# Fetching u for the S5 branch from another queue, and the order of VectorE's last steps before it

## Chip, cores and metric

The kernel runs on one core of a Trainium2 chip. The metric is the device time of one execution in microseconds, the median of several. A core has five engines that work side by side, each through its own instructions in order: TensorE (PE in the profile, matmuls), VectorE (DVE), ScalarE (ACT), GpSimd (POOL) and SyncE (SP, which only starts DMAs here). They meet at semaphores. The queue of an engine can also hold instructions that start a DMA; the profile marks SyncE's as SPq.

## What is computed

Two layers of a hybrid decoder trunk over 512 tokens of width 1024. Each layer is half a SwiGLU step, a mixing step with four branches, and another half SwiGLU step. This case plays at the start of mixing, where the normed input h is projected and the S5 branch begins:

```python
h = rms_norm(x, mix_norm[l])
p = h @ w_in[l]
p_m2, p_s5, p_dsa, p_hg = jnp.split(p, IN_SPLITS, axis=-1)
...
def s5_branch(u, ...):                       # u is p_s5, 512 columns in 32 groups of 16
    ug = u.reshape(b, L, S5_GROUPS, S5_GROUP)
    bu_re = jnp.einsum("blgi,gpi->blgp", ug, bb_re)
    bu_im = jnp.einsum("blgi,gpi->blgp", ug, bb_im)
    ...                                      # a scan over time, then y, gelu and a gated product
```

All arithmetic is float32. Each large product is made of three matmuls on split operands: x is written as x_hi + x_lo and w as w_hi + w_lo, with hi rounded to the matmul's own format, and hi times hi, lo times hi and hi times lo are summed.

## The kernel before

**Weight lots.** All weights come as a stream of lots, 512 KB each, numbered through a layer: 68 for the first SwiGLU step (MIX0 = 68), then the lots of mixing, then those of the second SwiGLU step. SP loads lot n into one of four slots of the tile raw (`load_lot`, L1074 in the profile, or the loop `ring`, L1107). ScalarE rounds it to w_hi (`split_hi`, L425). Then w_lo = raw - w_hi is made by VectorE or GpSimd (`split_lo`, L433), which counts `lo_done`; TensorE begins a lot when this count is there (`begin`). `lot_after(n)` on SP waits until lot n-4 has been split, since the slot is then free.

**The order of the steps** is a list, SCRIPT, that each engine's program walks through, doing its own part of each step. It begins: s5_w 0, quad u, s5_w 1, lot ks, lot q0, turn_small, q1, q2, s5_in, q3, k0, s5_out, k1, and so on. Lots: u is MIX0 to MIX0+3, ks MIX0+4, q0 MIX0+5, q1 MIX0+6, q2 MIX0+7.

- **quad u**: TensorE makes four output tiles of u from unnormed x, tile by tile of the eight k tiles. Meanwhile VectorE's `normalise_h` (L1814) makes the normed tiles, ScalarE rounds each to h_hi (L1488) and VectorE makes h_lo of it (`rest`, L1820). Afterwards VectorE reads the four banks of u times rstd into s5_uc (`keep_u`, L1826), with the columns reordered by time step.
- **s5_w 1**: TensorE transposes small matrices (L721), ScalarE copies them to s5_w (L1495), four copies here, eight in all.
- **lot ks** is the first gemm on the normed h: it waits for h_lo tile by tile. ScalarE evacuates its bank in three copies (L1415 to L1417), and the last frees the bank.
- **turn_small** (TensorE, L688): waits until ks is evacuated and until all eight s5_w copies are made, then does four tiny transposes (L693).
- **s5_in** (TensorE, L725): waits for `s5_u_in` (eight fetches of u), for s5_w and for ScalarE's copy of turn_small's result, then runs 128 small matmuls (L733).

**The way of u** over DRAM: SP writes s5_uc, one DMA for each of four tiles (L1150), into s5_ud, and fetches it back in another layout into s5_u, eight DMAs of 128 KB (L1157), one for each of the eight time steps of a block. Before the fetches it waits for all four writes. Two weight lots, MIX0+8 and MIX0+9, are loaded in between: one ahead of fetch 0, one ahead of fetch 4; MIX0+10 and MIX0+11 follow.

**On VectorE** the last steps of `normalise_h` are: keep_u(0), keep_u(1), the w_lo split of lot ks, keep_u(2), keep_u(3), rest(6), rest(7). **On ScalarE** quad ends with the splits of lots n+5, n+6 and n+7 (n = MIX0), and s5_w 1 follows. **GpSimd** in quad waits for the w_lo split of lot ks, then makes w_lo of lots n+5, n+6 and n+7 as their w_hi come.

Of the kernel before, what the change touches and what calls it, by code (L numbers as in the profile page):

```python
# [10 lines left out]
KT = DM // P  # L11
# [7 lines left out]
S5_Q, S5_CH = 8, 64  # L19
# [182 lines left out]
def trunk(nc, x_in, positions, w_lots, par_in, s5_in, con_in, gamma_in, out, s5_taps, s5_ud):  # L202
# [5 lines left out]
    with ctx:  # L208
# [159 lines left out]
        S = {}  # L368
# [58 lines left out]
        def split_lo(eng, n0, it=0):  # L427

            if isinstance(it, int) and n0 >= NLOT and OUT.layer == DEPTH - 1:
                return  # L430
            s = slot(n0)
            eng.wait_ge(S["hi_done"], 4 * it + (n0 + 1 + OUT.layer * NLOT))
            eng.tensor_tensor(w_lo[:, s], raw[:, s], w_hi[:, s].bitcast(f32), SUB).then_inc(S["lo_done"], 1)  # L433
# [633 lines left out]
        @block.sync  # L1067
        def _(sp):

            upper, freq = CON_AT["blk"], CON_AT["invfreq"]  # L1070

            def load_lot(layer, n):
                s = (layer * NLOT + n) % 4
                sp.dma_start(raw[:, s].rearrange("p k m -> p (k m)"), w_lots[layer * NLOT + n]) \  # L1074
                  .then_inc(S["raw_in%d" % s], 16)

            def load_par(layer):
                sp.dma_start(par[:, :], par_in[layer]).then_inc(S["par_in"], 16)

            def load_x(k):  # L1080
                sp.dma_start(x[:, k], x_in[k]).then_inc(S["c_x%d" % k], 16)

            def load_first(k):

                done = S["raw_in%d" % (k // 2)] if k % 2 else S["c_x%d" % k if k else "c_w0"]
                sp.dma_start(raw_k[:, k].rearrange("p j m -> p (j m)"), w_lots[k // 2][:, 4 * P * (k % 2):4 * P * (k % 2 + 1)]) \
                  .then_inc(done, 16)

            load_x(0)
            load_par(0)  # L1090
            load_first(0)
            for k in range(1, KT):
                load_x(k)
                load_first(k)
            sp.dma_start(con[:, 0:upper], con_in[:, 0:upper]).then_inc(S["c_ones"], 16)
            sp.dma_start(pos_i[:, :], positions.partition_broadcast(P)).then_inc(S["c_pos"], 16)
            sp.dma_start(con[:, freq:NCON], con_in[:, freq:NCON]).then_inc(S["c_pos"], 16)
            sp.dma_start(gam[:, :, :], gamma_in).then_inc(S["c_pos"], 16)
            for layer in range(DEPTH):
                OUT.layer = layer  # L1100

                def ring(first, to):
                    with sp.Fori(first, to) as it:
                        for n in range(4):

                            sp.wait_ge(S["lo_done"], it * 4 + LOT(n - 3))
                            sp.dma_start(raw[:, slot(n)].rearrange("p k m -> p (k m)"),  # L1107
                                         w_lots[layer * NLOT + it * 4 + n]).then_inc(S["raw_in%d" % slot(n)], 16)

                def lot_after(n):  # L1110

                    sp.wait_ge(S["lo_done"], LOT(n - 3))
                    load_lot(layer, n)

                def halves_across(g):

                    wait_taken(sp, out_at("qk"[g], 3))
                    for i in range(4):
                        to, of = slice(32 * i, 32 * i + 32), slice(32 * (i ^ 1), 32 * (i ^ 1) + 32)
                        sp.dma_start(da_s[to].rearrange("p j s -> p (j s)"),  # L1120
                                     da_qk[of, 4 * g:4 * g + 4].rearrange("p j s -> p (j s)")).then_inc(S["da_shifted"], 16)

                if layer:

                    sp.wait_ge(S["lo_done"], LOT(4))
                    sp.wait_ge(S["mix_clear"], 1)
                ring(1, 3)
                if layer == 0:
                    sp.dma_start(con[:, upper:freq], con_in[:, upper:freq]).then_inc(S["c_rest"], 16)
                sp.dma_start(s5_bc[:, :, :, :].rearrange("p a b c -> p (a b c)"), s5_in[layer, :, 0:1024]) \  # L1130
                  .then_inc(S["s5_in"], 16)
                sp.dma_start(s5_bp[:, :, :, :].rearrange("p a b c -> p (a b c)"), s5_in[layer, :, 1024:2048]) \
                  .then_inc(S["s5_in"], 16)
                ring(3, MIX0 // 4)
                sp.wait_ge(S["s5_tap_d"], 4)
                taps = s5_taps.rearrange("i (j g) c -> g i j c", g=8)
                for g in range(8):
                    sp.dma_start(taps[g], s5_tap[16 * g:16 * g + 16]).then_inc(S["s5_tap_out"], 16)
                ring(MIX0 // 4, MIX0 // 4 + 2)

                sp.wait_ge(S["s5_tap_out"], 16 * 8)
                sp.wait_ge(S["out_done"], OUT[MIX0])
                for i in range(S5_Q):
                    sp.dma_start(s5_t[16 * i:16 * i + 16], s5_taps[:, :, P - 16 * i:2 * P - 16 * i]) \
                      .then_inc(S["s5_taps_in"], 16)
                turn = FFN2_0 // 4 + 3
                for i in range(4):

                    wait_taken(sp, out_at("u", i))
                    sp.dma_start(s5_ud[P * i:P * (i + 1)], s5_uc[:, i]).then_inc(S["s5_u_out"], 16)  # L1150
                next_lot = MIX0 // 4 * 4 + 8
                sp.wait_ge(S["s5_u_out"], 16 * 4)
                u_by_step = s5_ud.rearrange("(g i) t c -> t i g c", i=16)
                for t in range(S5_Q):
                    if t % 4 == 0:
                        lot_after(next_lot + t // 4)
                    sp.dma_start(s5_u[16 * t:16 * t + 16], u_by_step[t]).then_inc(S["s5_u_in"], 16)  # L1157
                for n in (2, 3):
                    lot_after(next_lot + n)
                ring(MIX0 // 4 + 3, MIX0 // 4 + 4)  # L1160
                next_lot = MIX0 // 4 * 4 + 20
                for n in (-4, -3, -2):
                    lot_after(next_lot + n)
                sp.wait_ge(S["s5_y"], 2)
                halves_across(0)
                for n in (-1, 0, 1):
                    lot_after(next_lot + n)
                sp.wait_ge(S["da_rope"], 4)
                halves_across(1)
                for n in (2, 3):  # L1170
                    lot_after(next_lot + n)
                ring(MIX0 // 4 + 6, turn)

                sp.wait_ge(S["h_done"], H(H_RAW[2] + KT))
                if layer < DEPTH - 1:
                    load_par(layer + 1)
                ring(turn, NLOT // 4)
                for n in range(NLOT // 4 * 4, NLOT):
                    lot_after(n)
                for n in range(NLOT, NLOT + 4 if layer < DEPTH - 1 else NLOT):  # L1180

                    sp.wait_ge(S["lo_done"], LOT(n - 3))
                    load_lot(layer + 1, n - NLOT)
            n = NLOT - KT
            for i in range(KT - 1):
                wait_taken(sp, OUT[n + i])
                sp.dma_start(out[i], x[:, i]).then_inc(S["e_out"], 16)
            for half in range(2):
                tok = slice(2 * P * half, 2 * P * (half + 1))
                wait_taken(sp, OUT[n + KT - 1] + half)  # L1190
                sp.dma_start(out[KT - 1][:, tok], x[:, KT - 1, tok]).then_inc(S["e_out"], 16)
            sp.wait_ge(S["e_out"], 16 * (KT + 1))
# [78 lines left out]
        def _(act):  # L1271
# [203 lines left out]
            def quad(kind, i):  # L1475

                n = LOT_AT[(kind, i)]
                rstd_of(1)
                for k in range(KT):
                    if k == KT - 2:  # L1480
                        split_hi(act, n + 4)
                    act.wait_ge(S["normed_ready"], k + 1)
                    if k < KT - 1:

                        act.wait_ge(S["h_step"], k + 1)
                    else:
                        wait_out(act, OUT[n] + 3)
                    act.activation(h_hi[:, k], normed[:, k % 2], AFT.Copy).then_inc(S["h_hi_done"], 1)  # L1488
                for j in range(1, 4):
                    split_hi(act, n + 4 + j)  # L1490

            def s5_w_(phase):
# [291 lines left out]
        def _(dve):  # L1784
# [29 lines left out]
            def normalise_h():  # L1814
# [20 lines left out]
                keep_u(0)  # L1835
                keep_u(1)
                split_lo(V, MIX0 + 4)
                keep_u(2)
                keep_u(3)
                rest(KT - 2)  # L1840
                rest(KT - 1)

            def ffn(which, nb):
                n, g0 = nb, G(which)
# [718 lines left out]
```

## Time and profile before

| | us |
|---|---|
| median of 3 runs | 2822.57 (2822.3 to 2822.82) |
| the profiled execution | 2822.68 |
| its span in the trace | 2820.9 |
| TensorE busy | 2813.4 |
| VectorE busy | 1590.5 |
| ScalarE busy | 1185.5 |
| GpSimd busy | 707.0 |

The span is the time from the first to the last instruction of the profiled execution; the device time has 1.8 us around it. Busy time counts instructions that compute; register, semaphore and DMA-starting instructions aren't counted. Times of the trace are microseconds from the span's start. The two layers pass the place of the change at about 400 us and at about 1805 us.

### The profile page before, as it was taken

What the parts mean: (1) busy time and instruction counts of PE and PEld (TensorE: products, weight loads), DVE (VectorE), ACT (ScalarE), POOL (GpSimd) and SP (SyncE); (2) the same over time, 40 slices, a digit from 0 to 9 for tenths busy, and PEclk for the clock granted to TensorE, in tenths of its full rate; (3) what the DMA queues carried; (4) which work ended last, traced back from release to release, by engine and by line L of the source; (5) the groups of instructions that cost most, each with busy time, mean ns of one, the idle gap of its engine ahead of it and who ended that gap; (6) DMA issues with size and microseconds to landing.
All of it is one profiled execution on the core that took longest, in us unless ns stands there. A gap on an engine that the chain in (4) does not pass through costs nothing.

```text
span 2820.9 us, 38653 instructions
## 1 busy us (share of the span) xinstructions
PE 2813.4 (100%) x14306; PEld 2301.0 (82%) x14306; DVE 1590.5 (56%) x2316; ACT 1185.5 (42%) x1715; POOL 707.0 (25%) x336
## 2 busy tenths in 40 slices
PE   9999999999999999999999999999999999999999
PEld 8888888877788888888888888887777888888888
DVE  5584557685557454343544845576856673543434
ACT  5342354555355344232443423446553653442322
POOL 0085023333333440000000840234333334400000
PEclk9999999999999999999999999999999999999999
DMA  5333393222222232333233333932222222333332
GB/s 196 97 95 99 105 149 113 77 74 75 75 83 90 85 99 94 98 98 95 97 127 97 95 95 113 152 99 83 75 75 75 83 83 90 96 97 97 96 97 90
DMA packets 94242, 275.73 MB, mean 98 GB/s; under 512 B 17824, under 2 KB 27552, under 8 KB 93600
## 3 DMA queue, kind: packets, MB, share of 16 engines
q1 hardware_dynamic: 94112, 273.95, 33.6%
q8 instruction: 87, 1.43, 0.2%
q14 instruction: 43, 0.35, 0.0%
HBM read 264.48 MB, written 5.24 MB: 96 GB/s over the span
## 4 chain that ended last, share of the span: by engine, by line
PE 97%; DVE 2%; ACT 0%; DMA 0%; issue 0%; SPq 0%; ACTq 0%; DVEq 0%
PE bank L498 29%; PE bank L499 29%; PE bank L500 28%; PE bank L526 1%; PE bank L528 1%; PE bank L527 1%; PE bank L825 1%; PE bank L844 1%; PE bank L859 1%; PE bank L594 1%; PE bank L958 1%; PE bank L799 0%; DVE h_lo L1820 0%; PE bank L1016 0%; DVE s_uc L1826 0%; PE bank L1028 0%
## 5 line engine op out<-in xcount | busy, mean ns | idle before, releaser
L498 PE MATMUL bank<-h_hi,w_hi 128*128 128x512 f32 x2480 | 976.6, 394 | 2.7 <-DVE h_lo L1820 2.3
L500 PE MATMUL bank<-h_hi,w_lo 128*128 128x512 f32 x2480 | 965.6, 389 | 0.0
L499 PE MATMUL bank<-h_lo,w_hi 128*128 128x512 f32 x2480 | 965.5, 389 | 0.0
L425 ACT ACTIVATE w_hi<-raw 128x1024 fp32r<-128x1024 f32 x478 | 503.8, 1057 | 899.9 <-PE bank L500 879.8
L433 POOL TENSOR_TENSOR w_lo<-raw,w_hi 128x1024 fp32r<-128x1024 f32 x208 | 520.4, 2506 | 1091.7 <-ACT w_hi L425 1091.6
L498 PEld LDWEIGHTS bank<-h_hi,w_hi 128*128 128x128 f32 x2480 | 465.6, 188 | 107.7 <-issue 8.8
L500 PEld LDWEIGHTS bank<-h_hi,w_lo 128*128 128x128 f32 x2480 | 465.6, 188 | 97.9
L499 PEld LDWEIGHTS bank<-h_lo,w_hi 128*128 128x128 f32 x2480 | 465.8, 188 | 95.2 <-issue 1.7
L433 DVE TENSOR_TENSOR w_lo<-raw,w_hi 128x1024 fp32r<-128x1024 f32 x270 | 357.6, 1325 | 269.5 <-ACT w_hi L425 269.3
L498 PE MATMUL bank<-g_hi,w_hi 128*128 128x512 f32 x698 | 272.0, 390 | 0.0
L499 PE MATMUL bank<-g_lo,w_hi 128*128 128x512 f32 x698 | 271.6, 389 | 0.0
L500 PE MATMUL bank<-g_hi,w_lo 128*128 128x512 f32 x698 | 271.6, 389 | 0.0
L1856 DVE TENSOR_TENSOR gated<-bank,rstd 128x512 f32<-128x512 f32 x88 | 60.7, 690 | 216.8 <-PE bank L500 216.8
L1216 POOL TENSOR_TENSOR s_mag<-s_k,con 128x1024 f32<-128x1024 f32 x2 | 3.8, 1906 | 655.7 <-DVE s_k L2010 655.7
L1852 DVE TENSOR_TENSOR silu_a<-bank,rstd 128x512 f32<-128x512 f32 x88 | 60.7, 689 | 169.0 <-PE bank L500 147.1
L498 PEld LDWEIGHTS bank<-g_hi,w_hi 128*128 128x128 f32 x698 | 131.0, 188 | 28.6 <-DVE g_lo L1862 1.4
L500 PEld LDWEIGHTS bank<-g_hi,w_lo 128*128 128x128 f32 x698 | 131.0, 188 | 27.3
L499 PEld LDWEIGHTS bank<-g_lo,w_hi 128*128 128x128 f32 x698 | 131.0, 188 | 26.9
L498 PE MATMUL bank<-y_hi,w_hi 128*128 128x512 f32 x256 | 101.5, 396 | 0.0
L500 PE MATMUL bank<-y_hi,w_lo 128*128 128x512 f32 x256 | 99.8, 390 | 0.0
L499 PE MATMUL bank<-y_lo,w_hi 128*128 128x512 f32 x256 | 99.7, 389 | 0.0
L1466 ACT ACTIVATE gate_th<-bank 128x512 f32<-128x512 f32 x64 | 38.0, 593 | 140.4 <-PE bank L500 140.4
(373 smaller groups left out, 3366.3 us busy)
## 6 DMA issues: line engine op xcount, KB each, us to landing
raw<-in_w_lots SPq DMA_DIRECT2D x478, 512.0 KB, 3.6
s_t<-s_taps SPq DMA_DIRECT2D x16, 256.0 KB, 13.7
da_s<-da_qk SPq DMA_DIRECT2D x16, 256.0 KB, 4.1
x<-in_x SPq DMA_DIRECT2D x8, 256.0 KB, 5.3
raw_k<-in_w_lots SPq DMA_DIRECT2D x8, 256.0 KB, 5.6
s_ud<-s_uc SPq DMA_DIRECT2D x8, 256.0 KB, 4.2
s_u<-s_ud SPq DMA_DIRECT2D x16, 128.0 KB, 8.8
out_x<-x SPq DMA_DIRECT2D x7, 256.0 KB, 2.0
```

The source lines that it names most:

```text
L425: act.activation(w_hi[:, s], raw[:, s], AFT.Copy).then_inc(S["hi_done"], 1)
L433: eng.tensor_tensor(w_lo[:, s], raw[:, s], w_hi[:, s].bitcast(f32), SUB).then_inc(S["lo_done"], 1)
L498: pe.matmul(b[:, :], w_hi[:, s, kw], xh[:, k], start=(k == 0), stop=False)
L499: pe.matmul(b[:, :], w_hi[:, s, kw], xl[:, k], start=False, stop=False)
L500: return pe.matmul(b[:, :], w_lo[:, s, kw], xh[:, k], start=False, stop=(k == nk - 1))
L526: pe.matmul(o, h_hi[:, k, tok], wh[:, :, k], start=(k == 0), stop=False)
L527: pe.matmul(o, h_lo[:, k, tok], wh[:, :, k], start=False, stop=False)
L528: m = pe.matmul(o, h_hi[:, k, tok], wl[:, :, k], start=False, stop=(k == KT - 1))
L594: return pe.matmul(bank[j][:, :], w[:, k, j], h[:, k], start=(k == which == 0), stop=(k == KT - 1 and which == 2))
L1466: act.activation(gate_th[:, i % 2], bank[t % 4][:, :], AFT.Tanh, scale=0.5).then_inc(S["free%d" % (t % 4)], 1)
L1852: V.tensor_tensor(silu_a[:, q], bank[ta % 4][:, :], rstd[:, :], MUL).then_inc(S["free%d" % (ta % 4)], 1)
L1856: V.tensor_tensor(gated[:, q], bank[tb % 4][:, :], rstd[:, :], MUL).then_inc(S["free%d" % (tb % 4)], 1)
```

## The change

Three edits, each done in both layers.

1. SP no longer waits for the four writes of u and no longer starts the eight fetches; after the writes it loads lots MIX0+8 to MIX0+11, each when its slot is free.
2. ScalarE, at the end of quad, makes the split of lot n+5, then waits for the four writes, then starts the eight fetches, and only then makes the splits of lots n+6 and n+7.
3. VectorE does rest(6) and rest(7) (the last two h_lo tiles) ahead of keep_u(2) and keep_u(3).

```diff
--- before.py
+++ after.py
@@ -1149,13 +1149,7 @@
                     wait_taken(sp, out_at("u", i))
                     sp.dma_start(s5_ud[P * i:P * (i + 1)], s5_uc[:, i]).then_inc(S["s5_u_out"], 16)
                 next_lot = MIX0 // 4 * 4 + 8
-                sp.wait_ge(S["s5_u_out"], 16 * 4)
-                u_by_step = s5_ud.rearrange("(g i) t c -> t i g c", i=16)
-                for t in range(S5_Q):
-                    if t % 4 == 0:
-                        lot_after(next_lot + t // 4)
-                    sp.dma_start(s5_u[16 * t:16 * t + 16], u_by_step[t]).then_inc(S["s5_u_in"], 16)
-                for n in (2, 3):
+                for n in range(4):
                     lot_after(next_lot + n)
                 ring(MIX0 // 4 + 3, MIX0 // 4 + 4)
                 next_lot = MIX0 // 4 * 4 + 20
@@ -1486,7 +1480,12 @@
                     else:
                         wait_out(act, OUT[n] + 3)
                     act.activation(h_hi[:, k], normed[:, k % 2], AFT.Copy).then_inc(S["h_hi_done"], 1)
-                for j in range(1, 4):
+                split_hi(act, n + 5)
+                act.wait_ge(S["s5_u_out"], 16 * 4)
+                u_by_step = s5_ud.rearrange("(g i) t c -> t i g c", i=16)
+                for t in range(S5_Q):
+                    act.dma_start(s5_u[16 * t:16 * t + 16], u_by_step[t]).then_inc(S["s5_u_in"], 16)
+                for j in (2, 3):
                     split_hi(act, n + 4 + j)
 
             def s5_w_(phase):
@@ -1835,10 +1834,10 @@
                 keep_u(0)
                 keep_u(1)
                 split_lo(V, MIX0 + 4)
+                rest(KT - 2)
+                rest(KT - 1)
                 keep_u(2)
                 keep_u(3)
-                rest(KT - 2)
-                rest(KT - 1)
 
             def ffn(which, nb):
                 n, g0 = nb, G(which)
```

## Rows read from the trace of the kernel before

**Rows 1.** The page's busy time of each engine: us, share of the span, instructions.

```profile
PE 2813.4 (100%) x14306; PEld 2301.0 (82%) x14306; DVE 1590.5 (56%) x2316; ACT 1185.5 (42%) x1715; POOL 707.0 (25%) x336
```

**Rows 2.** Who waited for whom, engine PE, its longest: us in total, times, longest.

```profile
PE bank L498 <- DVE h_lo L1820: 2.3, 2, 1.1
```

**Rows 3.** Timeline of PE, first layer: start us, us, what [idle before <-releaser].

```profile
393.97 1.91 PE L721 MATMUL bank<-con,s_pre 128*128 128x128 f32 x16
395.63 0.48 PE L498 MATMUL bank<-h_hi,w_hi 128*128 128x512 f32 x1
...
401.80 0.50 PE L498 MATMUL bank<-h_hi,w_hi 128*128 128x512 f32 x1 [1.14 <-DVE h_lo L1820]
...
408.16 0.41 PE L693 MATMUL bank<-con,small_t 12*128 12x12 f32 x4
...
419.61 3.95 PE L733 MATMUL bank<-s_u,s_w 128*64 128x64 f32 x128
```

**Rows 4.** Timeline of PE, second layer.

```profile
1806.89 0.50 PE L498 MATMUL bank<-h_hi,w_hi 128*128 128x512 f32 x1 [1.13 <-DVE h_lo L1820]
...
1813.24 0.41 PE L693 MATMUL bank<-con,small_t 12*128 12x12 f32 x4
```

**Rows 5.** Timeline of DVE, first layer (xN: N instructions merged).

```profile
389.45 0.69 DVE L1820 TENSOR_TENSOR h_lo<-normed,h_hi 128x512 fp32r<-128x512 f32 x1 [0.40 <-ACT h_hi L1488]
...
394.06 2.16 DVE L1826 TENSOR_TENSOR s_uc<-bank,rstd 128x512 f32<-128x512 f32 x2
396.11 5.63 DVE L1820 TENSOR_TENSOR h_lo<-normed,h_hi 128x512 fp32r<-128x512 f32 x2
```

**Rows 6.** Timeline of POOL, first layer.

```profile
395.98 8.02 POOL L433 TENSOR_TENSOR w_lo<-raw,w_hi 128x1024 fp32r<-128x1024 f32 x3 [146.16 <-ACT w_hi L425]
```

**Rows 7.** Groups of DVE, shapes apart: busy us, mean ns | idle before.

```profile
L1953 DVE TENSOR_TENSOR merged<-merged,gate_th 128x512 f32<-128x512 f32 x48 | 43.0, 895 | 1.7
...
L1947 DVE SCALAR_TENSOR_TENSOR gate_th<-gate_th,bank 128x512 f32<-128x512 f32 x48 | 32.9, 684 | 93.9 <-PE bank L500 93.7
```

**Rows 8.** Timeline of ACT, first layer.

```profile
393.54 1.32 ACT L1488 ACTIVATE h_hi<-normed 128x512 fp32r<-128x512 f32 x2 [2.40 <-PE bank L500]
394.76 2.94 ACT L425 ACTIVATE w_hi<-raw 128x1024 fp32r<-128x1024 f32 x3
397.61 2.04 ACT L1495 ACTIVATE s_w<-bank 128x512 f32<-128x512 f32 x4
402.80 0.59 ACT L1415 ACTIVATE small_t<-bank 12x512 f32<-12x512 f32 x1 [3.15 <-PE bank L500]
```

**Rows 9.** SP's queue, first layer, and the landing times of line L1157.

```profile
396.25 0.61 SPq L1150 DMA_DIRECT2D s_ud<-s_uc  x1
...
400.03 0.34 SPq L1074 DMA_DIRECT2D raw<-in_w_lots  x1
400.41 2.02 SPq L1157 DMA_DIRECT2D s_u<-s_ud  x4
402.48 1.86 SPq L1074 DMA_DIRECT2D raw<-in_w_lots  x1
404.38 3.95 SPq L1157 DMA_DIRECT2D s_u<-s_ud  x4
...
407.14 1.19 SPq L1157 DMA_DIRECT2D s_u<-s_ud  x1
...
DMA to landing us min/median/max: 5.7/8.8/10.9
```

**Rows 10.** SP's queue: the s_t fetches together, and the fifth.

```profile
372.84 12.06 SPq L1144 DMA_DIRECT2D s_t<-s_taps  x8
...
375.52 2.02 SPq L1144 DMA_DIRECT2D s_t<-s_taps  x1
```

**Rows 11.** PE at the start, and the stretch's busy us, count, clock, DMA share, GB/s.

```profile
1.06 5.49 PE L588 MATMUL bank<-gated 128*128 128x128 f32 x24 [1.06 <-DVE roundc L2383]
...
1.10:6.50 5.40, 5.40 (x24) 1.00 0.70 236
```

## The prediction

> **What bounds the kernel now.** I read the page's busy times first: TensorE is busy for 2813.4 us of a 2820.9 us span [rows 1]. So the time is TensorE's own work, and a change to queues can only remove or add idle time of TensorE. Next I read what TensorE waited for. Its largest entry is two waits for h_lo tiles, 2.3 us together [rows 2]; these are all that this change aims at, out of 7.5 us of idle time in all. Then I read the engines side by side around the first layer's h_lo wait, at 400 to 402 us. TensorE runs the transposes of s5_w from 393.97, the lot ks from 395.63, and stands still for 1.14 us before the matmul at 401.80; it comes to the small transposes of turn_small (L693) at 408.16 and to s5_in at 419.61, neither with a wait [rows 3]. The second layer has the same picture: an idle time of 1.13 us, and L693 at 1813.24 [rows 4].
>
> Why is the last h_lo tile late? VectorE makes the last two tiles as its last work, from 396.11, and needs 5.63 us for two [rows 5], though the ones before take 0.69 us each [rows 5]. GpSimd's three w_lo splits run from 395.98 for 8.02 us, 2.67 us each [rows 6], and each h_lo ends about when one of those does. The Trainium skill (SBUF — State Buffer, "Who interferes with whom") states that VectorE with two SBUF inputs and GpSimd exclude each other for a whole instruction, and that VectorE with one SBUF input is free of this. The trace agrees in both halves: the two-input add of L1953 takes 895 ns on average, while the one of L1947 with a PSUM input takes 684 ns over the same stages [rows 7].
>
> **The VectorE half of the change.** rest(6) and rest(7) move ahead of keep_u(2) and keep_u(3). The w_lo split before them ends at 394.14 (the start of keep_u(2) in the row is 394.06, as neighbouring instructions overlap a little) [rows 5]. ScalarE's last two h_hi tiles run 393.54 to 394.86 [rows 8]. So the two h_lo run from about 394.2 to 395.6, ahead of GpSimd's first split at 395.98, at 0.69 us each. The last is there 5 us before TensorE asks for it: its idle time began at 401.80 - 1.14 = 400.7. The wait goes: **minus 1.1 us in each layer**. In exchange keep_u(2) and keep_u(3) end 2 x 0.69 = 1.4 us later, at 397.6 in place of 396.2. They read one PSUM bank and one SBUF tile, so by rows 7 GpSimd doesn't stretch them. The banks that they free are wanted by q1 and q2, over 10 us later; that costs nothing.
>
> **The queue half.** Before, SP waits for the four writes of u to DRAM: the last is issued at 396.25 and SP goes on at 400.03 [rows 9]. With keep_u(3) 1.4 us later this becomes 401.4. Now it is ScalarE that waits there, after its second split (lot n+5), and then issues eight fetches. Everything behind them on ScalarE waits as well: the splits of lots n+6 and n+7, the four s5_w copies, and the three evacuations of ks. Before, these ran from 394.8 on, with 3.15 us of idle time ahead of the ks evacuation [rows 8].
>
> What do eight issues cost on ScalarE? The trace shows none there, so I take SP's. The first four u fetches took 2.02 us together; a lot behind them then stood for 1.86 us, and the next four took 3.95 us, the last 1.19 us alone [rows 9]. The eight s_t fetches in a row, of twice the bytes, took 12.06 us: the fifth alone stood for 2.02 us after the first four had gone quickly [rows 10]. I read this as a queue that takes about four such fetches and then lets one in for each that drains. For ScalarE's queue: four at 0.49 with gaps 2.0; the fifth stands until 3.9 us after the first (on SP 404.34 minus 400.41, where the lot took that place); three more at 1.15 are 3.5. Together **7.4 us**. The lower bound, if nothing ever stands, is 8 x 0.49 = 3.9 us (nearest row: the first four); the upper is the s_t row, 12.1 us; near zero is the case below in which an issue is cheap on ScalarE. I take 7.4, since the bytes and row sizes are those of the u rows.
>
> Sum for ScalarE: 401.4 + 7.4 = 408.8; two weight splits at 0.98 (2.94 for three), four s5_w copies 2.04, three ks evacuations of 0.59 each, 1.8: 5.8 more [rows 8], so 414.6. TensorE, now 1.1 us earlier, comes to turn_small at 407.0. That step waits for ks to be evacuated and for the eighth s5_w copy. It **stands for 7.6 us**. Before, the same evacuation was done at 402.80 + 1.8 = 404.6, which left 3.6 us of slack; that cover is eaten by the later start and the issues. Net per layer 7.6 - 1.1 = 6.5, both layers 12.9 us.
>
> What else is queued: lot n+6's split comes at 409.8 and GpSimd's part 2.7 us later, 412.5; q1 can start only at about 415.0, so this is hidden under the stall with 2.5 us to spare. SP, freed of its wait, loads lots MIX0+8 and +9 from 398.7 on (that one needs GpSimd's first split, done at 398.65); lot MIX0+10 waits for the split at 412.5, and k1, which uses it, runs some 30 us later. Only bytes already on the way share the DMA engines with u. The fetches land by 408.8 + 10.9 = 419.7 at the latest (longest landing in the line's row, [rows 9]); s5_in, pushed to about 426, doesn't wait. The removal of the fetches from SP brings nothing by itself, as TensorE waits for no lot around it [rows 3].
>
> **The clock.** A stall of 7.6 us is longer than any in this trace: the longest named is 1.14 us, and the matmul after it takes 0.50 us, hardly more than the 0.48 us of the one that follows s5_w with no idle time [rows 3]. What a long rest does is only seen at the start. There the 24 small matmuls from 1.06 on take 5.49 us, 0.229 us each [rows 11]; 16 of the same shape in the middle take (395.63 - 393.97) / 16 = 0.104 us [rows 3]. So the array starts at half pace, though the granted-clock column reads 1.00 there too [rows 11]. A restart costs 5.49 - 24 x 0.104 = 3.0 us. I take it as the price after each stall: 2 x 3.0 = 6.0 us; the bounds are 0 (as after 1.14 us) and 3.0. The Trainium skill (TensorE: Matmul & The Clock Gate, "What's actually happening") states that an array that has rested is fed at 1.2 GHz, and at 2.4 GHz again once it has been kept busy. By that rule the price is paid; without it the sum would stay at 12.9 us.
>
> Forecast: 12.9 + 6.0 = **18.9 us more**. The profiled execution took 2822.68 us (span 2820.9 and 1.8 around it), 0.1 us over the median of 2822.57. So **2841.5 us**. About 0.2%, or 5.6 us, is what a measurement of this kernel can tell from no change.
>
> **Rivals.**
> - **The clock doesn't fall** in the stall: 2822.6 + 12.9 = 2835.5 us. For it: the column never moves in this trace. Against it: the pace at the start.
> - **The queue never stands.** ScalarE's issues cost 8 x 0.49 = 3.9 us, as SP's first four did. Stall 401.4 + 3.9 + 5.8 - 407.0 = 4.1, net 3.0 a layer and at most little clock loss: 2828.6 to 2834.6, with 2828.6 for the plain case. For it: ScalarE has a queue of its own, free of lots. Against it: the s_t row, also free of lots, stood from the fifth on.
> - **Not slower: issues on ScalarE are nearly free.** One number decides, the time X that the eight issues hold ScalarE. Stall is X + 0.2, net X - 0.9 per layer, so below X = 0.9 us the change gains. With X = 0.4 (0.05 each) it is 2 x 0.5 less: 2821.6 us; at X = 0 it is 2820.8. The Trainium skill (DMA: Bandwidth & Descriptors, "Issuing engines are not separate DMA queues") says that the time to start a DMA on a sequencer is usually small beside the DMA itself, and that only this time is saved or moved. By that rule X could be nearly nothing; here the row gives 0.43 to 1.19 us of issue beside a median of 8.8 us to landing, small in share and yet large beside 3.6 us of slack.
> - **The queue drains as slowly as for s_t:** 12.1 us for eight, stall 12.3, net 11.2 a layer and 6.0 for the clock: 2851 us.
> - That the change doesn't do what it says would be h_lo waits that stay; then each case is 2.3 us higher. I see no way to it, as the tiles' inputs are there at 394.9.
>
> **How the numbers follow.** Chances: forecast 0.45, no clock fall 0.20, queue never stands 0.17, not slower 0.12, slow drain 0.06. The range from 2828.0 to 2845.0 leaves out the last two, 0.18, and takes in the others with a few us for the size of X. Within 0.2% is up to 2828.2: the 0.12 of cheap issues and about a third of the 0.17, as 2828.6 is at the edge, together 0.18. Faster by over 0.2% would need 5.6 us, most of TensorE's 7.5 us of idle time, of which the waits named give 2.3: 0.01. Slower: 0.81.
>
> **What would show it.** In the profile after: the two h_lo about 0.69 us each before 396 us, and no TensorE wait on them; eight issues on ScalarE's queue from about 401.4, four quick and four slow, ending near 408.8; an idle time of TensorE of about 7.6 us before L693, put down to ScalarE's ks evacuation; after it matmuls of doubled spacing for some us. If ScalarE's issues end by 402.3, or TensorE isn't idle before L693, the sum is wrong at X; if the stall is there at even pace, the clock term is wrong.

## The result

| | before | changed |
|---|---|---|
| median of 6 runs, us | 2822.89 (2822.3 to 2823.68) | 2839.32 (2836.37 to 2840.35) |
| profiled execution / its span, us | 2822.68 / 2820.9 | 2838.92 / 2836.9 |
| TensorE busy, us | 2813.4 | 2817.2 |

The changed kernel is slower by about half a per cent: ratio 1.0056, 95% interval 1.0045 to 1.0066. The forecast was 2841.5 us, and 2839.32 lies within its range of 2828.0 to 2845.0. Its span is 16.0 us longer, and TensorE's busy time rose by only 3.8 us of that; the rest is idle time. From its page: the busy times, and the queue that is new (packets, MB, share of 16 engines).

```profile
PE 2817.2 (99%) x14306; PEld 2304.4 (81%) x14306; DVE 1582.2 (56%) x2316; ACT 1185.4 (42%) x1715; POOL 705.4 (25%) x336
...
q10 hardware_dynamic: 8448, 2.10, 1.1%
```

It is ScalarE's queue, and moves 2.10 MB, the sixteen fetches. Who waited for whom, engine PE (us in total, times, longest):

```profile
PE bank L693 <- ACT da_ki L1411: 14.3, 2, 7.6
```

The h_lo waits of [rows 2] are gone, and a wait of 14.3 us for ScalarE's last ks evacuation stands in their place. TensorE's timeline in the first layer, the answer to [rows 3]:

```profile
406.46 0.39 PE L500 MATMUL bank<-h_hi,w_lo 128*128 128x512 f32 x1
414.44 0.59 PE L693 MATMUL bank<-con,small_t 12*128 12x12 f32 x4 [7.60 <-ACT da_ki L1411]
...
415.56 0.63 PE L499 MATMUL bank<-h_lo,w_hi 128*128 128x512 f32 x1
...
418.97 0.47 PE L498 MATMUL bank<-h_hi,w_hi 128*128 128x512 f32 x1
419.28 0.39 PE L499 MATMUL bank<-h_lo,w_hi 128*128 128x512 f32 x1
...
428.01 3.95 PE L733 MATMUL bank<-s_u,s_w 128*64 128x64 f32 x128
```

The last matmul of q0 starts at 406.46, and turn_small at 414.44, after 7.60 us of idle time; in [rows 3] it started at 408.16. From 415.56 to 418.97 the matmuls follow each other at 0.43 us, eight steps, and from 419.28 at 0.23 again. s5_in comes at 428.01 in place of 419.61. The second layer:

```profile
1827.05 0.60 PE L693 MATMUL bank<-con,small_t 12*128 12x12 f32 x4 [6.73 <-ACT da_ki L1411]
...
1840.84 3.95 PE L733 MATMUL bank<-s_u,s_w 128*64 128x64 f32 x128
```

Idle 6.73 us; turn_small to s5_in is 13.79 us, 11.45 before. ScalarE in the first layer, the answer to [rows 8], with its DMA issues as ACTq:

```profile
394.84 1.04 ACT L425 ACTIVATE w_hi<-raw 128x1024 fp32r<-128x1024 f32 x1
400.60 7.93 ACTq L1487 DMA_DIRECT2D s_u<-s_ud  x8
408.62 1.06 ACT L425 ACTIVATE w_hi<-raw 128x1024 fp32r<-128x1024 f32 x1 [12.74 <-issue]
...
413.80 0.59 ACT L1411 ACTIVATE da_ki<-bank 64x512 f32<-64x512 f32 x1
```

And three of the eight issues by themselves, the second, the fifth and the last:

```profile
400.98 0.50 ACTq L1487 DMA_DIRECT2D s_u<-s_ud  x1
...
402.73 1.74 ACTq L1487 DMA_DIRECT2D s_u<-s_ud  x1
...
407.13 1.39 ACTq L1487 DMA_DIRECT2D s_u<-s_ud  x1
```

ScalarE rests from 395.9 to 400.60, where it waits for the four writes, issues for 7.93 us, and only then makes the two splits, four copies of s5_w and the three evacuations that had been over by 404.6. VectorE and GpSimd, the answers to [rows 5] and [rows 6]:

```profile
394.28 1.37 DVE L1819 TENSOR_TENSOR h_lo<-normed,h_hi 128x512 fp32r<-128x512 f32 x2
```

```profile
396.06 2.41 POOL L433 TENSOR_TENSOR w_lo<-raw,w_hi 128x1024 fp32r<-128x1024 f32 x1 [146.21 <-ACT w_hi L425]
```

The two h_lo take 1.37 us together and end before GpSimd's split begins. Busy time of TensorE, count, granted clock, DMA share and GB/s by stretches (the DMA share can read over 1; nothing here rests on it):

```profile
407.00:410.00 3.00, 0.00 (x0) 0.82 1.44 89
410.00:414.00 4.00, 0.00 (x0) 0.50 1.45 96
416.00:418.00 2.00, 2.00 (x6) 0.50 0.93 365
420.00:422.00 2.00, 2.00 (x10) 1.00 0.87 195
```

The granted clock goes from 1.00 (2.4 GHz) to 0.50 (1.2 GHz) while TensorE stands idle (0.82 on average from 407 to 410, 0.50 from 410 to 414), is still 0.50 from 416 to 418, with TensorE at work again, and is back at 1.00 from 420 to 422. The slow stretch of work lasts from 414.44 to about 419.1, some 4.7 us.

### The profile page after: what moved, and what is told of

Read it like the earlier page. It is cut to its first block, busy times and chain, and to the rows that moved or that the text cites. A ratio compares the mean times of both kernels' runs of the same rounds, so it can differ in the third digit from the quotient of the medians.

```text
span 2836.9 us, 38651 instructions
## 1 busy us (share of the span) xinstructions
PE 2817.2 (99%) x14306; PEld 2304.4 (81%) x14306; DVE 1582.2 (56%) x2316; ACT 1185.4 (42%) x1715; POOL 705.4 (25%) x336
## 4 chain that ended last, share of the span: by engine, by line
PE 97%; DVE 1%; ACT 1%; ACTq 1%; DMA 1%; issue 0%; SPq 0%; DVEq 0%
PE bank L498 29%; PE bank L500 28%; PE bank L499 28%; PE bank L526 1%; PE bank L528 1%; PE bank L527 1%; PE bank L825 1%; PE bank L844 1%; PE bank L859 1%; PE bank L594 1%; PE bank L958 1%; ACTq L1487 1%; PE bank L799 0%; PE bank L1016 0%; PE bank L1028 0%
```

## The experiments

Each kernel ran interleaved with the kernel before on one chip; medians of 5 to 11 runs, the kernel before at 2823.41 in the first group (runs 1, 2, 3a, 4), 2822.54 in the second (3b, 5, 6, 7) and 2822.77 in the third (8 to 11). My theory from the trace of the changed kernel: ScalarE, held by its wait and by the issues, delays what TensorE needs at turn_small; the clock adds a little; VectorE's half is innocent. The rivals: the later u, the transfers, or the wait rather than the issues. The changed kernel ran only beside its own kernel before (2822.89), so a difference to it compares runs of two groups.

### 1. VectorE's half alone

```diff
 # the kernel before
                 split_lo(V, MIX0 + 4)
+                rest(KT - 2)
+                rest(KT - 1)
                 keep_u(2)
                 keep_u(3)
-                rest(KT - 2)
-                rest(KT - 1)
```

> The kernel before with only VectorE's order changed; SP keeps its wait and the eight fetches. My theory: the h_lo waits (2.3 us) go and nothing of the changed kernel's loss is here, as ScalarE is held by nothing: 2820.6 us. The u writes end about 1 us later, so the last fetch is issued near 409 us and lands up to 10 us on, near 419, while s5_in comes at 418.5: up to 1 us of new wait per layer is possible, 2822.6 at most. Rival (the later u is what costs in the changed kernel): several us over the time before, 2830 or more.

Measured: 2822.56 us, ratio 0.9994 (0.9985 to 1.0003). The loss is not here. Of the gain of 2.3 us that I expected the medians show 0.9, but the interval is too wide to tell a full gain from none. TensorE's waits, and s5_in in the first layer, show what works against it:

```profile
PE bank L733 <- DMA s_u<-s_ud: 4.6, 2, 3.0
...
419.41 3.95 PE L733 MATMUL bank<-s_u,s_w 128*64 128x64 f32 x128 [1.68 <-DMA s_u<-s_ud]
```

No h_lo wait; in its place 4.6 us of waiting for u at s5_in (1.68 us in one layer, 2.95 us in the other). This profiled execution is the slowest of the eleven (2825.18, the fastest 2820.36), so the waits are at the upper end of what they are. I had allowed up to 1 us per layer; it was more. The kernel before had little slack for u, and I hadn't looked for it, since slack leaves no wait in a trace. It can be read from the landing times of the eight fetches, counted from each one's start. First layer of the kernel before:

```profile
DMA to landing us min/median/max: 5.7/8.7/10.4
```

The longest, 10.4 us, is the last one's. It starts at 407.14 [rows 9], so u is there at about 417.5, and s5_in starts at 419.61: 2.1 us of slack. In the second layer the last fetch starts at 1812.7 and takes 10.9 us, and s5_in starts at 1824.69: 1.1 us. Here, in the first layer, TensorE was at s5_in at 417.7, and the last fetch, started at 407.53, took 11.8 us to land, until 419.3.

### 2. The queue half alone

```diff
 # the changed kernel
                 split_lo(V, MIX0 + 4)
-                rest(KT - 2)
-                rest(KT - 1)
                 keep_u(2)
                 keep_u(3)
+                rest(KT - 2)
+                rest(KT - 1)
```

> The changed kernel with VectorE's old order. My theory: ScalarE's chain alone sets when TensorE goes on after turn_small, so the h_lo wait of 1.1 us falls inside the same stall and the two halves don't add up: the writes of u end up to 1.4 us earlier, ScalarE's eight issues take 8 us again, TensorE stands for 5 to 6 us from 408.2, the clock term of 2.1 to 2.3 us is paid in both layers: 2837 to 2839 us. Rival (the halves add up): the changed kernel's 2839.3 plus 2.3 is 2841.6 us. Rival (the loss comes from VectorE's half): near 2823.

Measured: 2839.16 us, ratio 1.0052 (1.0038 to 1.0066), the same as both halves together. So the whole loss is the queue's. Waits of TensorE, and then from the first layer ScalarE's issues and VectorE's last two h_lo:

```profile
PE bank L693 <- ACT da_ki L1411: 17.7, 2, 9.2
...
402.22 7.71 ACTq L1487 DMA_DIRECT2D s_u<-s_ud  x8
...
395.98 3.44 DVE L1819 TENSOR_TENSOR h_lo<-normed,h_hi 128x512 fp32r<-128x512 f32 x2
```

No h_lo wait is left here either, though VectorE has its old order: ScalarE makes only one split before it waits, so GpSimd has only one to make beside the two h_lo, and these take 3.44 us in place of 5.63. TensorE began to stand at 406.65 (turn_small at 415.85, less 9.20), about as in the changed kernel (406.84), and not at 408.2 as I had expected. So beside the queue's half VectorE's half had nothing left to gain: the queue's half takes away the collision by itself.

This profiled execution took 2842.72 us, 3.6 over the median. If that excess lay in these waits, their usual sum is nearer 14 us (an estimate); I had expected 10 to 12. ScalarE's first fetch came at 402.22 instead of earlier than in the changed kernel, though the last write of u was started 1.7 us sooner: the writes took longer to land (median 6.1 us, against 4.3). Lots were started right behind them in both kernels, and in run 11, where none were, the median is 5.6 us; why they took longer here stays open.

### 3. The clock by itself

```diff
 # the changed kernel, TensorE
             def turn_small():
 
+                t = out_at("q", 1)
+                pe.wait_ge(S["free%d" % (t % 4)], t // 4)
+                for i in range(62):                  # 28 in the second run
+                    pe.matmul(bank[t % 4][:, 0:P], ident, ones, start=True, stop=True)
                 wait_taken(pe, out_at("ks", 0))
```

> The changed kernel with 62 matmuls of 128x128 float32 on constants ahead of turn_small's waits, into a bank that q1 overwrites; about 6.7 us of work in the time in which TensorE stood. What is computed stays. My theory: the stall's length stays, as ScalarE sets it, but the array is not at rest and its clock stays up, so the slow stretches behind the stalls (2.1 and 2.3 us) go: 2839.3 - 4.4 = 2834.9 us. Rival (the slow stretch has another cause, such as contention with the fetches): no gain, 2839 us.

Measured (3a): 2847.45 us. My size was wrong: a float32 matmul of 128x128 is two records of 0.11 us, so 62 of them are 14.0 us of work per layer, more than the stall. This run can't be the test, as TensorE's own added work is now what delays turn_small. With 28:

> The run before this with 62 matmuls ahead of turn_small overshot, as each float32 matmul shows as two in the trace and takes 0.226 us: 14.0 us of work in a stall of 7. Now 28 matmuls, 6.3 us, shorter than both stalls. What is computed stays. My theory: ScalarE still sets when turn_small starts, 0.4 to 1.3 us of idle time are left, and the clock stays up: the changed kernel less 2.1 and 2.3 us, so 0.15% below it; with the changed kernel at 2839.3 that is 2834.9 us. Rival (the slow stretch comes from contention with the transfers): 2839 us.

Measured (3b): 2833.8 us, ratio 1.0040 (1.0026 to 1.0054), 5.5 us less than the changed kernel's 2839.3, where I had expected 4.4. The two ratio intervals overlap a little (the changed kernel's begins at 1.0045), the times don't (2833.24 to 2835.46, against 2836.37 to 2840.35); the profiled executions differ by 4.1 us. TensorE's timeline and stretches, first layer:

```profile
406.37 6.41 PE L693 MATMUL bank<-con 128*128 128x128 f32 x56
413.01 0.41 PE L697 MATMUL bank<-con,small_t 12*128 12x12 f32 x4 [0.23 <-ACT da_ki L1415]
...
424.45 3.72 PE L737 MATMUL bank<-s_u,s_w 128*64 128x64 f32 x120
...
412.00:414.00 2.00, 1.77 (x14) 1.00 0.58 229
```

The added matmuls run from 406.37, turn_small at 413.01, s5_in 11.44 us later (11.45 before the change, 13.57 in the changed kernel), with the clock at 1.00 throughout. In the second layer it is 11.46 us, against 13.79. ScalarE still sets when turn_small starts, though not at the same time as in the changed kernel: its issues took 6.85 us in the first layer and 9.12 in the second, so turn_small came 6.6 and 8.5 us after the added matmuls began. What the test turns on is the stretch behind it: without rest it isn't slow. The clock term is shown by it, 2.1 and 2.3 us of the 16.0.

### 4. Only the wait on ScalarE, the issues on SP

```diff
 # the changed kernel, ScalarE; SP gets a wait and the eight fetches ahead of its lots
                 act.wait_ge(S["s5_u_out"], 16 * 4)
-                u_by_step = s5_ud.rearrange("(g i) t c -> t i g c", i=16)
-                for t in range(S5_Q):
-                    act.dma_start(s5_u[16 * t:16 * t + 16], u_by_step[t]).then_inc(S["s5_u_in"], 16)
```

> The changed kernel, but ScalarE only waits for the four writes of u and starts no DMA; SP waits for them too and starts the eight fetches in one block ahead of the lots. It parts the wait from the issues. My theory: ScalarE goes on at 400.6, its 5.8 us of work end at 406.5, and TensorE comes to turn_small at 407.0: no or hardly any stall, 2820.6 to 2821.5 us. Rival (the wait on ScalarE is the harm, whoever issues): a stall of several us and over 2830. Rival (eight fetches in a block are the harm): s5_in waits for u, over 2825.

Measured: 2820.71 us, ratio 0.9986 (0.9977 to 0.9995): 18.6 us less than the changed kernel. Waits of TensorE, and SP's eight fetches:

```profile
PE bank L693 <- ACT da_ki L1415: 0.5, 1, 0.5
...
399.57 4.82 SPq L1155 DMA_DIRECT2D s_u<-s_ud  x8
```

The wait costs 0.5 us in one layer; the issues are what costs. Unlooked for: the eight took 4.82 us on SP, where ScalarE had needed 7.93.

### 5. Four fetches on each queue

```diff
 # the changed kernel; SP waits for the writes and issues fetches 4 to 7 ahead of its lots
-                for t in range(S5_Q):
+                for t in range(4):
                     act.dma_start(s5_u[16 * t:16 * t + 16], u_by_step[t]).then_inc(S["s5_u_in"], 16)
```

> The changed kernel with only four of the eight fetches on ScalarE; SP waits for the writes too and issues the other four, ahead of its lots. My theory (a queue takes about four such fetches quickly): ScalarE is held for 2.1 us, its chain ends at 400.1 + 2.1 + 5.9 = 408.1, TensorE stands 0.7 to 1.7 us per layer from 406.9, too short for the clock to fall: 2822 to 2824 us. Rival (the issues stand because the DMA engines behind both queues are full): the two queues hold each other, ScalarE is held for 4 us or more and the time is over 2826 us.

Measured: 2824.74 us (2821.53 to 2829.11), ratio 1.0007 (0.9997 to 1.0016).

```profile
PE bank L693 <- ACT da_ki L1415: 4.5, 2, 2.9
...
400.79 2.00 ACTq L1491 DMA_DIRECT2D s_u<-s_ud  x4
...
400.78 1.91 SPq L1155 DMA_DIRECT2D s_u<-s_ud  x4
```

Both queues took their four within 2.0 us at the same time, so the quick start of four isn't shared between the queues, and the stalls shrank from 14.3 to 4.5 us. They were longer than the 0.7 to 1.7 us that I had expected in one layer, 1.59 and 2.86 us. Wrong was, too, that such stalls are too short for the clock. After 1.59 us of rest, first layer:

```profile
408.71 0.41 PE L693 MATMUL bank<-con,small_t 12*128 12x12 f32 x4 [1.59 <-ACT da_ki L1415]
...
410.56 0.63 PE L500 MATMUL bank<-h_hi,w_lo 128*128 128x512 f32 x1
...
408.00:410.00 2.00, 1.29 (x8) 1.00 1.02 236
410.00:412.00 2.00, 2.00 (x7) 0.51 1.02 403
```

The matmuls go on at the quick pace, turn slow from about 410 on, and stay slow to about 413 us; behind the rest of 2.86 us they are slow as well. That a rest as short as this is itself the cause isn't tested; run 3b tests it for the long ones. (This execution is the slowest of eleven; the fastest, at 2821.53, can't have paid this in both layers.)

### 6. The fetches behind the evacuation of ks

```diff
 # the changed kernel, ScalarE: wait and fetches taken out of quad
                     act.activation(da_ki[64:128, :], src[0:64, :], AFT.Copy).then_inc(S["free%d" % (t % 4)], 1)
                     split_hi(act, n + 4)
+                    act.wait_ge(S["s5_u_out"], 16 * 4)
+                    u_by_step = s5_ud.rearrange("(g i) t c -> t i g c", i=16)
+                    for t in range(S5_Q):
+                        act.dma_start(s5_u[16 * t:16 * t + 16], u_by_step[t]).then_inc(S["s5_u_in"], 16)
```

> The changed kernel with ScalarE's wait and eight fetches moved behind its evacuation of ks and the split that follows, so that turn_small's inputs are ready first. My theory (what counts is what stands behind the issues on ScalarE): no stall at turn_small, the fetches run from 404.5 on and take 5 to 8 us; the last lands at 418 to 421, against s5_in at 418.0: 0 to 3 us of wait for u per layer, 2820.6 to 2826.6 us, my value 2823. Rival (fetches from ScalarE's queue are slow in themselves, and u comes late whatever their place): over 2830 us.

Measured: 2824.39 us (2820.52 to 2827.79), ratio 1.0005 (0.9996 to 1.0014).

```profile
PE bank L733 <- DMA s_u<-s_ud: 2.8, 2, 2.5
...
403.43 8.39 ACTq L1416 DMA_DIRECT2D s_u<-s_ud  x5
```

No wait at turn_small; what is left is 2.8 us for u. The place of the issues on ScalarE is worth 15 us. The eight took even longer here, the last five alone 8.39 us. SP had all four lots on the way by then (started from 398.19 on, within 5.31 us), which may be why; no run tests it at this place.

### 7. The lots behind u

```diff
 # the changed kernel, SP
+                sp.wait_ge(S["s5_u_in"], 16 * S5_Q)
                 for n in range(4):
                     lot_after(next_lot + n)
```

> The changed kernel with one more wait on SP: lots MIX0+8 and later are loaded only when all of u has landed. Eight fetches stay on ScalarE. In the kernel in which SP issued the eight in a block ahead of the lots they took 4.8 us on SP's queue, against 7.5 to 8.0 us on ScalarE's in the changed kernel, where 1 MB of lots goes ahead. Theory A (the lots ahead hold up the draining): ScalarE is held for about 4.8 us, the stall is 400 + 4.8 + 5.9 - 406.9 = 3.8 us, 2822.9 - 2.3 + 7.6 = 2828.2 us, up to 2832.6 if the clock still falls. Theory B (ScalarE's queue is slower in itself): 7.5 to 8.0 us again and 2839 us.

Measured: 2835.84 us (2832.45 to 2838.08), ratio 1.0045 (1.0032 to 1.0059).

```profile
PE bank L693 <- ACT da_ki L1412: 11.4, 2, 6.8
...
399.88 5.50 ACTq L1488 DMA_DIRECT2D s_u<-s_ud  x8
```

The issues take 5.50 us here (5.43 in the second layer), against 7.93 and 7.51. SP's blocks took 4.82 to 5.60 us in runs 4, 9, 10 and 11. So ScalarE's queue isn't slower than SP's: about 2 us of its 7.9 came with the lots that SP had started ahead. (With these lots ahead the eight took 6.85 to 9.12 us on ScalarE in the profiled executions of the changed kernel, run 2 and both runs of 3.) Theory A is right in kind: the issues are shorter. But the time is 3 us above its upper value, which already has the clock's fall in it. The step that was short is the stall: 4.65 and 6.77 us in place of 3.8 in each layer. The issues took 0.6 to 0.7 us longer than the 4.8 taken, and in the second layer ScalarE's wait ended 4.5 us after the last write's start, against 2.3 in the first.

### 8. GpSimd's splits behind the h_lo tiles

```diff
 # the kernel before, GpSimd in quad
                         pool.wait_ge(S["lo_done"], LOT(LOT_AT[step[1:]] + 5))
+                        pool.wait_ge(S["h_done"], H(2 * KT + KT))
```

> The kernel before, VectorE's and SP's order untouched; GpSimd waits for all eight h_lo tiles before its first split of quad u. It tests by itself why the last two h_lo took 2.8 us each. Theory (GpSimd's split, which reads and writes SBUF, keeps VectorE's two-input subtract out while it runs): the two h_lo run at 396.1 to 397.5 at 0.69 us each, no h_lo wait, 2820.6 us, or up to 2821.5 if s5_in then waits a little for u. Rival (the h_lo are slow for another reason, such as the transfers): 2.8 us each again and 2823 us or more.

Measured: 2820.80 us, ratio 0.9994 (0.9985 to 1.0003). VectorE's two h_lo and GpSimd's three splits, first layer:

```profile
395.70 1.31 DVE L1821 TENSOR_TENSOR h_lo<-normed,h_hi 128x512 fp32r<-128x512 f32 x2
...
397.25 7.10 POOL L433 TENSOR_TENSOR w_lo<-raw,w_hi 128x1024 fp32r<-128x1024 f32 x3 [148.08 <-DVE h_lo L1821]
```

At the same place in VectorE's order as in the kernel before, the two take 1.31 us in place of 5.63, and GpSimd's three take 7.10 in place of 8.02. That the two engines hold each other up is shown. The h_lo wait is gone; in the second layer of the profiled execution, 2.6 us over the median, a wait of 2.5 us for u came up instead.

### 9 to 11. The block of fetches on SP

```diff
 # the kernel before, SP
                 for t in range(S5_Q):
-                    if t % 4 == 0:
-                        lot_after(next_lot + t // 4)
                     sp.dma_start(s5_u[16 * t:16 * t + 16], u_by_step[t]).then_inc(S["s5_u_in"], 16)
-                for n in (2, 3):
+                for n in range(4):
                     lot_after(next_lot + n)
```

Run 9 has this and VectorE's new order, run 10 this alone, run 11 this and GpSimd's added wait of run 8.

> VectorE's new order, nothing moved to ScalarE, and SP issues the eight fetches in one block ahead of all lots. Theory: the h_lo waits go (2.3 us), no stall at turn_small, the fetches take 4.8 us on SP and land by 413, five us ahead of s5_in, so VectorE's half keeps its gain, which with lots in between it lost again to waits for u of 1.7 and 3.0 us: 0.08% under the kernel before, 2820.3 us. Rival (the earlier order of lots was needed): TensorE waits for a w_lo and the time is 2823 us or more.

> The kernel before with the eight fetches in one block ahead of lots MIX0+8 and +9 on SP, and nothing else. Theory: the h_lo waits stay, u was in time anyway, so no difference: within 0.5 us of the kernel before. Rival (the block itself brings the gain of the kernel in which ScalarE only waited): 2.3 us under it.

> The block of fetches on SP, VectorE's old order, and GpSimd's splits behind the h_lo tiles. Theory: the h_lo waits go by the other way and u isn't made later at all: 2.3 us under the kernel before, the same as with VectorE's new order and the block. Rival (GpSimd's later splits leave q0 without its w_lo): TensorE waits at about 401 us and the gain is lost.

Measured: run 9 2819.86 us, ratio 0.9987 (0.9978 to 0.9996); run 10 2822.70 us, 0.9996 (0.9987 to 1.0005); run 11 2820.29 us, 0.9988 (0.9979 to 0.9997). Run 9, SP's fetches and TensorE's steps in the first layer:

```profile
399.58 5.37 SPq L1155 DMA_DIRECT2D s_u<-s_ud  x8
...
406.34 0.41 PE L693 MATMUL bank<-con,small_t 12*128 12x12 f32 x4
...
417.79 2.43 PE L733 MATMUL bank<-s_u,s_w 128*64 128x64 f32 x75
```

Turn_small comes at 406.34 and s5_in at 417.79, with no wait at either; TensorE has no wait for h_lo or u left in this kernel. In run 10 one entry stays on top:

```profile
PE bank L498 <- DVE h_lo L1818: 2.3, 2, 1.1
```

The block alone brings nothing, VectorE's half alone little if anything, and the two together 0.13%: u has to be early enough to let TensorE come earlier. Run 9 is the fastest kernel measured here, 2.9 us under the kernel before and 19.5 under the changed one; run 11, and run 4 against its own kernel before (2.7 us), don't differ from it clearly.

## The prediction, step by step

**VectorE's half** was right as far as it went: two h_lo in 1.4 us, no wait, 1.1 us less per layer (with the slower first matmuls after it, TensorE reached the end of q0 1.4 us sooner, 406.46 against 407.84). In the changed kernel it counts for nothing, as run 2 shows: the stall ends when ScalarE is done, however early TensorE comes, and the queue's half removes the h_lo wait by itself, which I hadn't seen. My sum subtracted the gain from a stall that it had lengthened by the same amount, so the sum is right; as a gain it isn't there. That the later keep_u tiles cost nothing is true only while ScalarE stands longer than u needs; alone (run 1) they use up u's slack. The two rows by which the prediction supports the collision of VectorE and GpSimd (895 and 684 ns, [rows 7]) are of two different operations and show little; run 8 shows it, with the same two h_lo at 1.31 and 5.63 us.

**The wait's end**: forecast 401.4, measured 400.60. I had taken 3.8 us from the last write's start, and it was 2.8.

**The issues, X**: forecast 7.4 us, measured 7.93 and 7.51. The pattern of four quick and four slow is in the trace (0.50 us for the second, 1.74 for the fifth, 1.39 for the last), and run 5 shows the four quick ones on both queues at once. What I had not separated is the share of the lots ahead, about 2 us (run 7): the row of SP's that I took had them in between. And X moves between executions, from 6.85 to 9.12 us with the lots ahead, so that a single execution came within 0.5 us of the forecast is in part luck.

**The chain behind**, 5.8 us: measured 414.39 minus 408.52, 5.9.

**The stall**: forecast 7.6 us in both layers, measured 7.60 and 6.73. The first hits by luck: the wait ended 0.8 us early and the issues took 0.5 us more, and the 0.2 us that are left are made up by TensorE, which came at 406.84 in place of 407.0. In the second layer the wait ended 2.4 us after the last write's start and the issues were shorter.

**The clock**: right in kind, too large in size. The step taken from the start of the kernel, 3.0 us, was mis-sized: there 5.49 us of work ran at half pace, and behind the stall some 4.7 us in the first layer. Measured were 2.1 and 2.3 us (13.57 and 13.79 against 11.45 us from turn_small to s5_in), and run 3b takes them away.

Net, by the steps' own times: the first layer loses 6.28 us up to turn_small and 2.12 behind it, the second 5.41 and 2.34; together 16.15, of which 0.15 comes back later. Forecast 18.9: over by 1.5 us in the clock term and by 1.2 in the stalls, mostly the second layer's.

**The rivals**: no clock fall is refuted (the granted clock and the pace in the changed trace, and run 3b), cheap issues are refuted by the changed trace and run 4, an unlimited queue (3.9 us) and one as slow as for s_t (12.1 us) by the measured 7.93 and 7.51. The sentence of the Trainium skill that starting a DMA is usually small beside the DMA (DMA: Bandwidth & Descriptors, "Issuing engines are not separate DMA queues") would, taken as X nearly nothing, have led to the opposite sign. One issue is small here too, 0.32 to 1.74 us beside a median of 9.2 us to landing; but eight in a row held ScalarE for 7.93 us, against 3.6 us of slack, and by that the measurement decides. "The removal of the fetches from SP brings nothing by itself" held (run 10), and it hid something: u's way had only 1 to 2 us of slack, which runs 1 and 8 brought out.

## What to carry over

An issue on a compute engine's queue is an instruction like any other: price the whole train of them, with the rows of a queue that already stood, and compare with the slack of whatever lies behind on that engine. A wait that is removed is a gain only if the next input is there earlier as well; test the two together, since alone each may show nothing. And a transfer that lands in time, however barely, is in no list of waits: read its slack from its start and its landing time.

## What the runs showed of the hardware

- The clock fell behind rests far shorter than I had thought it needed: after 1.59 us of TensorE standing, the granted clock was 0.51 in the stretch from 410 to 412 us and the matmuls took 0.43 us each (run 5). After the rest of 1.14 us in the kernel before it stayed at 1.00 (402 to 408 us).
- The granted clock reads 1.00 at the very start, where 24 matmuls run at half pace [rows 11]. In the changed kernel the column and the pace agree, so at the start the pace is the better witness.
- Eight fetches of 128 KB took 4.82 us to issue on SP and 5.50 on ScalarE with no lots ahead, and 7.93 us on ScalarE with 1 MB of lots ahead (runs 4 and 7, the changed kernel); the quick start of four took about 2 us on either queue (run 5).
- GpSimd lost by the collision too: three splits in 8.02 us beside VectorE's subtracts, 7.10 us without (run 8).
